# Two transformer layers on one core: scan inputs of the second mixer as 128-row products, values as a feature tile, and preparations moved into the first feed-forward

## The chip, the cores and the metric

One Trainium2 chip, one of its cores. The metric is the time of one execution on the device in microseconds (us), median of three. The core has TensorE (PE, with its weight loads as PEld), VectorE (DVE), ScalarE (ACT), GpSimd (POOL) and SyncE (SP, which here only issues DMAs). All tensors are float32; most products are done as three passes of a split operand (below).

## The reference, cut to what matters

The program is two layers over 512 tokens with 1024 features. The first (a mixer of four kinds of attention and convolution, then a feed-forward of width 2816) matters here only as the place where work for the second is done. The second layer is modulated by a vector c, and half of its mixer is an S5 scan:

```
mod = silu(c) @ w_mod + b_mod          # 6 x 1024: shift1, scale1, gate1, shift2, scale2, gate2
h   = rms(x) * norm1 * (1 + scale1) + shift1
u, q, k, v = split(h @ w_in)           # 512 scan features, 512 of queries, 128 keys, 128 values
a   = exp(dt * (lam_re + i lam_im))    # one complex pole per state, 32 groups x 64 states
bb  = (a - 1) / lam * b                # per group: 16 inputs -> 64 states
s[l] = a * s[l-1] + bb @ u[l]          # the scan
y[l] = Re(c @ s[l]) + d * u[l]
attention of 8 query heads on 2 key heads, window 128, with a learned bias by distance
x = x + gate1 * (norm(glu(gelu(y))), norm(attention)) @ w_out
x = x + gate2 * feed_forward(rms(x) * norm2 * (1 + scale2) + shift2)
```

## The kernel before, in words

Features lie on partitions, tokens along the row; x is 8 tiles of 128 x 512. A weight chunk is 128 x 2048 (1 MB). SP loads it (`load_chunk`, L113) into one of two slots, ACT rounds it (`round_chunk`, L121), DVE takes the rest (`rest_chunk`, L127), and PE does `split_mm` (L133 to L135), three products per tile. Counting semaphores `w_loaded`, `w_hi`, `w_lo`, `w_used` pass a chunk on. The order of each engine's work is written out by hand; an engine does its list strictly in order, and there is a barrier of all engines between stages.

The first feed-forward (`FeedForward`, L243) runs in two halves of 11 up turns (each a chunk for two tiles, 48 products) and 8 down turns (33 products): 38 turns, numbered from 0. In an up turn DVE copies both banks out of PSUM with the norm's root, takes the rest of the chunk two ahead, multiplies gate and value and takes `hlo`, the rest of the rounded product, which the down turns need. In the last down turns ACT squares x and POOL adds for the norm r3 of the second layer.

Beside it runs `Modulation` (L382). Its matrix is cut into 16 chunks of 384 columns, each 8 row blocks: 128 steps on DVE (L432, L435), 4 per up turn, 3 per down turn, into a ring of six accumulators. PE sums a finished chunk over its partitions by three products with a column of ones (`reduce`, L445), two turns after its last step in the first half; six of the 16 sums come after the feed-forward. `finish_early` and `finish` add the bias, the latter in the second mixer. SP loads half a chunk (`load`, L413) when the half two back is used up. POOL computes the poles and, when ACT has moved two transposed tiles (`a_moved`), the B matrices times the powers 0 to 3 of the pole (L1387), where time is taken in chunks of TS = 4 steps.

The second mixer is the stage at L1805. PE's order: the first chunk of w_in2 with the shifted norm as it comes (`shifted_dve`, `shifted_act`), a small product for the distance bias, transposes of B, the second chunk, `inputs(0)`, the third chunk (one feature tile, and the values with tokens on the partitions: 96 products of 128 columns), `inputs(1)`, the fourth and fifth chunk, `lag_weights`, and the attention in 16 pairs `p`, with the scan's outputs (`lags`, `from_states`) put between. `inputs(pair)` (L2272) makes the chunk inputs of the scan: for each of two tiles, real and imaginary part, each of four steps t and each of four 32-row groups one product, with the input read at a stride of four. DVE turns them by the angles (`spin`), scans (`scan`, L2129) and turns back (`spin_back`). The angles come from `turns` (ACT), `angle` (DVE), `sines` (ACT) and `cosine` (DVE) in this stage, and POOL lifts C by the powers (L1923, L1940). SP (L1890) loads C, a time table and two tables for the bias, then a weight chunk, writes 8 rows of the bias 128 times over to DRAM (`rel_scratch`, L1902) and reads them back skewed (`bias2`, L1908). PE's `lags` and `from_states` write the output at a stride of four.

Of the kernel before, what the change touches and what calls it, by code (L numbers as in the profile page):

```python
# [381 lines left out]
class Modulation:  # L382
# [3 lines left out]
    EARLY = 6  # L386
    AT_END = 10
    UP, DOWN = 4, 3

    def __init__(self, k, io, sb, ctx, pr, mods, keep_sem):  # L390
# [4 lines left out]
        self.ready, self.step, self.early = k.sem("mod_c_ready"), k.sem("mod_step"), k.sem("mod_early")  # L395
        self.reduced = keep_sem("mod_reduced")
        self.loaded = [k.sem("mod_loaded0"), k.sem("mod_loaded1")]
        self.at = 0

# [18 lines left out]

    def multiply(self, dve, steps):

        for e in range(self.at, min(self.at + steps, 8 * self.N)):
# [7 lines left out]
            if j == 0:  # L429
                if c >= self.KEPT:  # L430
                    dve.wait_ge(self.reduced, c - self.KEPT + 1)
# [6 lines left out]
        self.at += steps  # L438

    def reduce(self, pe, c):  # L440
        pe.wait_ge(self.step, 8 * (c + 1))
        if c == self.EARLY:
            pe.wait_ge(self.early, 1)
# [5 lines left out]
    def reduce_after(self, pe, turn):  # L449

        for c in range(self.AT_END):
            if turn == (self.turn_of(8 * (c + 1)) + 2 if c < self.EARLY else HALF + KT + 3 + 2 * (c - self.EARLY)):
                self.reduce(pe, c)

    def finish_early(self, dve):
        dve.wait_ge(self.reduced, self.EARLY)
        dve.tensor_tensor(self.mods[:, 0:16], self.k.bank[7][:, 0:16], self.pr("b_mod")[:, 0:16], ALU.add)\
            .then_inc(self.early, 1)

    def finish(self, dve):  # L460
        dve.wait_ge(self.reduced, self.N)
        return dve.tensor_tensor(self.mods[:, 16:48], self.k.bank[7][:, 16:48], self.pr("b_mod")[:, 16:48], ALU.add)
# [133 lines left out]
def program(nc, io):  # L596
    root_ctx = ExitStack()
    with root_ctx:
# [728 lines left out]
        ffn_ctx = ExitStack()  # L1327
        a_rows = sb("a_rows", [P, 2, S], ctx=ffn_ctx)
        xhi = nc.alloc_sbuf_tensor_at("xhi_ffn1", [P, KT, S], R, offset=o_at)
        xlo = sb("xlo_ffn1", [P, KT, S], R, ffn_ctx)  # L1330
        modulation = Modulation(k, io, sb, ffn_ctx, pr, mods, keep_sem)
# [16 lines left out]
        def out_bank(t):  # L1348
# [4 lines left out]
        b_in, col_exp, col_sin, col_den, col_inv, a_made, a_turned, a_moved = (  # L1353
            k.sem(f"ssm_{w}") for w in ("b_in", "exponents", "sines", "denominator", "inverse", "wide", "turned", "rows"))
# [7 lines left out]
        with nc.Block() as block:  # L1362

            @block.sync
            def _(sp):
# [5 lines left out]
                    .then_inc(b_in, 16)  # L1371
                for n in range(GU, IN2 + 4):
                    load_chunk(sp, k, n % 2, ffn.source(n) if n < IN2 else io["w_in2"][IN2_AT[n - IN2]], after_lo=n - 1)
                    for half in range(2, 2 * modulation.N):
                        if modulation.turn_of(4 * (half - 1)) == n - GU - 4:
                            modulation.load(sp, half)

            @block.gpsimd
            def _(pool):
# [56 lines left out]
                for n in range(1, TS):  # L1436
                    was, now = (powers[:, m, :, :, :].rearrange("p a t n -> p a (t n)") for m in (n - 1, n))
                    for a, op in ((0, ALU.subtract), (1, ALU.add)):
                        tt(twist[:, 0, :], was[:, 0, :], a_rows[:, a, :], ALU.mult)
                        tt(twist[:, 1, :], was[:, 1, :], a_rows[:, 1 - a, :], ALU.mult)  # L1440
                        tt(now[:, a, :], twist[:, 0, :], twist[:, 1, :], op)
                for j in range(1, KT - 1):
                    r3.add(pool, k, j)
# [3 lines left out]
            def _(act):  # L1447
# [76 lines left out]

                for half in range(2):
# [5 lines left out]
                    for j in range(KT):  # L1531
                        if half == 1:
                            if j == 0:
                                act.preload_act_table_set("natural_log_exp_and_others")
# [9 lines left out]
            def _(dve):  # L1544
# [103 lines left out]

                for half in range(2):
                    for i in range(HALF * half, HALF * half + HALF):  # L1650
                        ffn.dve_up(dve, i, k.root[:, :], lambda: modulation.multiply(dve, modulation.UP // 2))
                    for j in range(KT):
# [4 lines left out]
                        if half == 0 and j == KT - 1:  # L1657
                            modulation.finish_early(dve)
                        if half == 1 and j == 1:
                            dve.wait_ge(modulation.early, 1)  # L1660
                            dve.scalar_tensor_tensor(out=scale1, in0=scale1, scalar=1.0, in1=pr("norm1"), op0=ALU.add,
                                                     op1=ALU.mult)
# [3 lines left out]
            def _(pe):  # L1666
# [109 lines left out]
                for half in range(2):  # L1776
                    for i in range(HALF * half, HALF * half + HALF):
# [11 lines left out]
                        modulation.reduce_after(pe, turn)  # L1789
                        turn += 1  # L1790
                    for j in range(KT):
                        ffn.pe_down(pe, half, j)
                        modulation.reduce_after(pe, turn)
                        turn += 1
                r3.pe_sum(pe, k, KT - 2, [KT - 1])
                for n in range(modulation.AT_END, modulation.N):
                    modulation.reduce(pe, n)
# [8 lines left out]
        bt = sb("b_turned", [P, 2, S], ctx=mix_ctx)  # L1806
        proj2 = sb("proj2", [P, 9, S], ctx=mix_ctx)
        v2 = sb("v2", [P, NT, P], ctx=mix_ctx)
        y = o_all
        lift = sb("c_lifted", [P, 2, 16, TS + 1, 32], ctx=mix_ctx)  # L1810
        circle = sb("cos_sin", [P, 16, 2, NCK], ctx=mix_ctx)
# [3 lines left out]
        kx2 = sb("kx2", [P, S], ctx=mix_ctx)  # L1815
        k.nmax = sb("nmax2", [P, 32], ctx=mix_ctx)
# [4 lines left out]
        ssm_c = over("ssm_c", [P, 2, 16, 32], bias_at)  # L1821
        time = over("time", [P, S], bias_at + 2 * TILE)
        hot = over("hot", [33, 384], bias_at + 3 * TILE)
# [6 lines left out]
        states = [over("states0", [P, 2, 8, NCK], raw_at + 4 * TILE),  # L1830
                  powers[:, 0:2, :, :, :].rearrange("p n a t c -> p n (a t) c")]
# [4 lines left out]
        hot_in, rel_made, rel_sb, rel_out, rel_in, c_taken, time_set = (  # L1836
            k.sem(w) for w in ("hot_in", "rel_made", "rel_copied", "rel_out", "rel_in", "ssm_c_taken", "time_set"))
        h3_scaled, h3_rounded, h3_split = k.sem("in2_scaled"), k.sem("in2_rounded"), k.sem("in2_split")
        evac2a, evac2v, half_made, c_in, bt_made, bt_sb, lifted, turned, angled, sined, half_sined, circled = (
            k.sem(w) for w in ("in2_stored_a", "in2_stored_v", "in2_half", "ssm_c_in", "b_turned", "b_copied", "c_lifted",  # L1840
                               "turns", "angles", "sines", "half_sines", "circle"))
# [12 lines left out]
        chunk_time = time[:, :].rearrange("p (c t) -> p c t", t=TS)[:, :, 0]  # L1854
        clock = k.bank[6][:, 0:NCK]
# [9 lines left out]
        SPIN_AT = (1, 3, 5, 7, 9, 11)  # L1865
# [929 lines left out]
```

## Time and profile before

| | us |
|---|---|
| median of three executions | 1278.69 (1277.31 to 1279.43) |
| the profiled execution, its own time | 1280.15 |
| span from its first to its last instruction | 1278.4 |
| PE busy in it | 1228.0 |
| mean granted clock of TensorE | 0.984 of full |

The page gives busy times by engine, the costliest groups of instructions and the DMA issues. A line of the timeline is one or several like instructions: start, length, engine, source line, operation, output and inputs, count, and in brackets the idle time of the engine ahead of it with what ended it. PE's products overlap in the records: the start of the next tells how long one took. PE's counts give two records for a float32 product of the scan or the attention. Some matmul records can be missing.

### The profile page before, as it was taken

To read this page: it belongs to the slowest core of one execution; us is meant where nothing else is said; L and a number is where in the kernel's file an instruction comes from. 1 tells how busy PE (TensorE), PEld (TensorE's weight loads), DVE (VectorE), ACT (ScalarE), POOL (GpSimd) and SP (SyncE) were. 2 spreads that over 40 slices of the span, in tenths; PEclk is the share of its full clock that TensorE was granted. 3 is DMA by queue.
4 is the path that set the end of the run, shared out by engine and by line. 5 is a ranking of instruction groups with operands and counts; after the bars stand their busy time and mean duration, and the time that the engine had idled before them with its cause. 6 is when DMAs were issued, how large, how long until landed. Compare 5 with 4: busy or idle time off the path is not lost. (4 is left out here: it accounts for less than half of the span.)

```text
span 1278.4 us, 15375 instructions
## 1 busy us (share of the span) xinstructions
PE 1228.0 (96%) x6230; PEld 964.9 (75%) x6230; DVE 762.3 (60%) x1224; ACT 485.6 (38%) x738; POOL 125.3 (10%) x124
## 2 busy tenths in 40 slices
PE   7999998899999999999997999879899999999998
PEld 5786665578888788888885785558688878888877
DVE  5536674755665865656555896846755652455542
ACT  5244545734322212222324814564433331333320
POOL 0000000014000800000010930014100000000000
PEclk9999999999999999999998998979899999999999
DMA  9311011222443365554443341102122223222222
GB/s 345 130 62 66 34 66 47 86 100 99 166 153 132 118 206 190 173 173 135 134 154 121 62 88 34 67 6 95 66 99 99 78 73 127 101 99 99 68 91 89
DMA packets 25829, 138.40 MB, mean 108 GB/s; under 512 B 2879, under 2 KB 5152, under 8 KB 16544
## 3 DMA queue, kind: packets, MB, share of 16 engines
q1 hardware_dynamic: 25760, 137.43, 32.0%
q8 instruction: 49, 0.80, 0.3%
q14 instruction: 20, 0.16, 0.0%
HBM read 133.75 MB, written 3.67 MB: 107 GB/s over the span
## 5 line engine op out<-in xcount | busy, mean ns | idle before, releaser
L133 PE MATMUL bank<-xhi_ffn,w_hi_part 128*128 128x512 f32 x704 | 278.1, 395 | 4.4 <-DVE xlo_ffn L233 4.4
L134 PE MATMUL bank<-xlo_ffn,w_hi_part 128*128 128x512 f32 x704 | 277.1, 394 | 0.0
L121 ACT ACTIVATE w_hi_part<-w_raw 128x2048 fp32r<-128x2048 f32 (+1 forms) x96 | 165.8, 1727 | 290.6 <-PE bank L135 288.9
L135 PE MATMUL bank<-xhi_ffn,w_lo_part 128*128 128x512 f32 x704 | 275.2, 391 | 0.0
L127 DVE TENSOR_TENSOR w_lo_part<-w_raw,w_hi_part 128x2048 fp32r<-128x2048 f32 (+1 forms) x96 | 198.4, 2067 | 111.8 <-ACT w_hi_part L121 107.6
L133 PEld LDWEIGHTS bank<-xhi_ffn,w_hi_part 128*128 128x128 f32 x704 | 133.0, 189 | 34.7 <-issue 5.4
L135 PEld LDWEIGHTS bank<-xhi_ffn,w_lo_part 128*128 128x128 f32 x704 | 132.8, 189 | 29.5
L134 PEld LDWEIGHTS bank<-xlo_ffn,w_hi_part 128*128 128x128 f32 x704 | 132.6, 188 | 28.0 <-issue 0.2
L360 DVE SCALAR_TENSOR_TENSOR squares<-bank,param,squares 128x511 f32<-128x511 f32 x88 | 63.9, 747 | 84.7 <-ACT squares L343 83.1
L133 PE MATMUL bank<-hhi,w_hi_part 128*128 128x512 f32 x240 | 94.5, 394 | 1.7 <-DVE hlo L368 1.7
L133 PE MATMUL bank<-hhi_half,w_hi_part 128*128 128x512 f32 x240 | 94.2, 392 | 0.7 <-DVE hlo_half L332 0.7
L134 PE MATMUL bank<-hlo,w_hi_part 128*128 128x512 f32 x240 | 93.4, 389 | 0.0
L134 PE MATMUL bank<-hlo_half,w_hi_part 128*128 128x512 f32 x240 | 93.4, 389 | 0.0
L135 PE MATMUL bank<-hhi,w_lo_part 128*128 128x512 f32 x240 | 93.4, 389 | 0.0
L135 PE MATMUL bank<-hhi_half,w_lo_part 128*128 128x512 f32 x240 | 93.4, 389 | 0.0
L435 DVE SCALAR_TENSOR_TENSOR mod_acc<-mod_w,mod_c,mod_acc 128x384 f32<-128x384 f32 x112 | 75.6, 675 | 2.7
L133 PE MATMUL bank<-xhi,w_hi_part 128*128 128x512 f32 x144 | 61.4, 427 | 8.4 <-DVE w_lo_part L954 7.4
L343 ACT ACTIVATE squares<-bank,param 128x512 f32<-128x512 f32 x44 | 31.9, 777 | 82.8 <-PE bank L135 82.8
L320 DVE TENSOR_TENSOR squares<-bank,rms_root 128x512 f32<-128x512 f32 x22 | 15.2, 691 | 79.7 <-PE bank L135 72.4
L135 PE MATMUL bank<-xhi,w_lo_part 128*128 128x512 f32 x144 | 57.3, 398 | 0.0
L134 PE MATMUL bank<-xlo,w_hi_part 128*128 128x512 f32 x144 | 56.9, 395 | 0.0
L133 PEld LDWEIGHTS bank<-hhi_half,w_hi_part 128*128 128x128 f32 x240 | 45.1, 188 | 12.8 <-issue 1.7
(363 smaller groups left out, 1928.5 us busy)
## 6 DMA issues: line engine op xcount, KB each, us to landing
mod_w<-in_w_mod SPq DMA_DIRECT2D x32, 768.0 KB, 4.4
w_raw<-in_w_gu SPq DMA_DIRECT2D x22, 1024.0 KB, 4.8
w_raw<-in_w_down SPq DMA_DIRECT2D x32, 704.0 KB, 4.1
w_raw<-in_w_up SPq DMA_DIRECT2D x22, 1024.0 KB, 4.8
w_raw<-in_w_in_f SPq DMA_DIRECT2D x8, 1024.0 KB, 5.1
w_raw<-in_w_out SPq DMA_DIRECT2D x8, 1024.0 KB, 4.9
w_raw<-in_w_in SPq DMA_DIRECT2D x5, 1024.0 KB, 4.8
x<-in_x SPq DMA_DIRECT2D x8, 256.0 KB, 6.5
```

The lines of the kernel that those rows point to most:

```text
L121: act.activation(k.whi[:, slot, 0:width], k.raw[:, slot, 0:width], ACT.Copy).then_inc(k.w_hi, 1)
L127: dve.tensor_tensor(k.wlo[:, slot, 0:width], k.raw[:, slot, 0:width], k.whi[:, slot, 0:width].bitcast(F), ALU.subtract).then_inc(k.w_lo, 1)
L133: pe.matmul(out, whi, xhi, start=first, stop=False)
L134: pe.matmul(out, whi, xlo, start=False, stop=False)
L135: return pe.matmul(out, wlo, xhi, start=False, stop=last)
L320: dve.tensor_tensor(gate, k.bank[a][:, :], root, ALU.mult).then_inc(self.gated, 1)
L343: act.activation(k.sq[:, s, :], k.bank[s][:, :], ACT.Identity, bias=bias[:, 2 * i + a:2 * i + a + 1], scale=taps[:, 6 * i + 3 * a + 2:6 * ...
L360: dve.scalar_tensor_tensor(out=y, in0=k.bank[s][:, 0:S - back], scalar=taps[:, tap:tap + 1], in1=y, op0=ALU.mult, op1=ALU.add).then_inc(se ...
L435: ins = dve.scalar_tensor_tensor(out=acc, in0=w, scalar=self.c[:, j:j + 1], in1=acc, op0=ALU.mult, op1=ALU.add)
```

## The change

- Modulation: 6 steps per up turn and 5 per down turn, so that step 128 falls in turn 22. PE sums four chunks at once into four 32-row groups of bank 7 (`reduce(m)`, each with a 32-column weight that holds a column of ones at place m), one turn after their last step (turns 6, 11, 17, 23). In turn 23 DVE copies the bank, in 24 PE transposes it and DVE adds the bias and forms both scales.
- The lift of C (POOL), the angles, sines and cosines (ACT, DVE) are done in the first feed-forward: POOL from turn 24, ACT and DVE in the last down turns. C and the time table are loaded there.
- `inputs(pair)`: the rows of the four steps are laid under each other by DMA from SBUF to SBUF, 32 DMAs for the powers at the stage's start, 16 per pair for the inputs; then 16 products of 128 rows per pair. The scan tiles of `proj2` are stored by step (t outer), so `lags` and `from_states` have no stride and the output of DVE has one.
- Values: 24 products of 512 columns into a feature tile, copied by ACT, four transposes by PE.
- `lag_weights` and ACT's copies of its result come right after `inputs(0)`; one third of a back rotation moves from pair 11 to ahead of the attention; the first `load` of SP comes after `rel_scratch`.

The core of the diff:

```diff
 class Modulation:
-    UP, DOWN = 4, 3
+    UP, DOWN = 6, 5
+    GROUP = 4
...
-    def reduce(self, pe, c):
-        pe.wait_ge(self.step, 8 * (c + 1))
...
-        for t in range(3):
-            mm = pe.matmul(self.k.bank[7][:, 3 * c + t:3 * c + t + 1], self.acc[:, c % self.KEPT, P * t:P * t + P],
-                           self.k.ones[:, 0:1], start=True, stop=True)
+    def reduce(self, pe, m):
+        pe.wait_ge(self.step, 8 * self.GROUP * (m + 1))
+        for q in range(self.GROUP):
+            mm = pe.matmul(self.k.bank[7][32 * q:32 * q + 32, 0:self.W], self.pick[:, 32 - m:64 - m],
+                           self.acc[:, (self.GROUP * m + q) % self.KEPT, :], start=(m == 0), stop=(m == 3))
         mm.then_inc(self.reduced, 1)
+    def pe_after(self, pe, turn):
+        for m in range(4):
+            if turn == self.turn_of(8 * self.GROUP * (m + 1)) + 1:
+                if m == 0:
+                    pe.wait_ge(self.picks, 2)
+                self.reduce(pe, m)
+        if turn == self.summed_at + 1:
+            pe.wait_ge(self.copied, 1)
+            for t in range(3):
+                mm = pe.transpose(self.k.bank[7][:, P * t:P * t + P], self.acc[:, 0, P * t:P * t + P], self.k.ident)
+            mm.then_inc(self.turned, 1)
...
 # first feed-forward, ACT, second half
                     for j in range(KT):
+                        if half == 0 or j < KT - 1:
+                            ffn.act_weights(act, ffn.down_chunk(half, j) + 2)
                         if half == 1:
...
                             r3.act_square(act, k, x[:, j, :], j)
-                        if half == 0 or j < KT - 1:
-                            ffn.act_weights(act, ffn.down_chunk(half, j) + 2)
+                            if j == 0:
...
+                                turns(0)
+                                turns(1)
+                            if j in (1, 2):
+                                turns(j + 1)
+                            if 2 <= j < 6:
+                                sines(j - 2)
...
                 r3.act_root(act, KT, eps_col[:, 0:1])
-                act.preload_act_table_set("trig_and_small")
...
 # DVE
+                            if 1 <= j < 5:
+                                angle(j - 1)
+                            if 3 <= j < 7:
+                                cosine(j - 3)
...
 # second mixer, SP
+                for pair in range(2):
+                    for t in range(TS):
+                        for q in range(4):
+                            sp.dma_start(b_rows[pair][rows_of(t), q, :, :, :],
+                                         powers[rows_of(q), TS - 1 - t, :, 2 * pair:2 * pair + 2, :])\
+                                .then_inc(b_rows_in[pair], 16)
+                def turn_inputs(pair):
+                    sp.wait_ge(evac2a, pair + 1)
+                    sp.wait_ge(evac2v, pair + 1)
+                    for t in range(TS):
+                        for q in range(4):
+                            sp.dma_start(u_rows[rows_of(t), 2 * pair:2 * pair + 2, q, :],
+                                         proj2[rows_of(q), 2 * pair:2 * pair + 2, NCK * t:NCK * t + NCK])\
+                                .then_inc(u_rows_in[pair], 16)
+                sp.wait_ge(b_rows_in[0], 256)
+                sp.wait_ge(b_rows_in[1], 256)
+                turn_inputs(0)
                 sp.wait_ge(rel_sb, 1)
                 sp.dma_start(io["rel_scratch"], rel_rows[:, :].unsqueeze(1).broadcast_to([8, P, 384])).then_inc(rel_out, 16)
+                load_chunk(sp, k, (IN2 + 4) % 2, io["w_in2"][IN2_AT[4]], after_lo=IN2 + 3)
+                turn_inputs(1)
...
 # PE
                 def inputs(pair):
-                    for b in (2 * pair, 2 * pair + 1):
+                    pe.wait_ge(b_rows_in[pair], 256)
+                    pe.wait_ge(u_rows_in[pair], 256)
+                    for b in range(2):
                         for a in range(2):
-                            for t in range(TS):
-                                for q in range(4):
...
-                                    mm = pe.matmul(in_banks[q][:, at:at + NCK], powers[r, TS - 1 - t, a, b, :],
-                                                   steps_of(r, b)[:, :, t], start=(t == 0), stop=(t == TS - 1))
+                            for q in range(4):
+                                at = NCK * (2 * b + a)
+                                mm = pe.matmul(in_banks[q][:, at:at + NCK], b_rows[pair][:, q, a, b, :],
+                                               u_rows[:, 2 * pair + b, q, :], start=True, stop=True)
                     mm.then_inc(v_made, 1)
...
                 features(IN2 + 1, 0).then_inc(half_made, 1)
-                pe.wait_ge(evac2v, 1)
-                features(IN2 + 1, 1).then_inc(k.w_used, 1)
                 pe.wait_ge(rel_sb, 1)
                 pe.wait_ge(bt_sb, 2)
                 inputs(0)
+                lag_weights()
+                pe.wait_ge(evac2v, 1)
+                features(IN2 + 1, 1).then_inc(k.w_used, 1)
+                pe.wait_ge(k.w_lo, IN2 + 3)
                 pe.wait_ge(evac2a, 2)
-                features(n, 0).then_inc(half_made, 1)
-                pe.wait_ge(evac2v, 2)
...
+                features(IN2 + 2, 0).then_inc(half_made, 1)
                 pe.wait_ge(v_turned, 4)
                 inputs(1)
+                pe.wait_ge(evac2v, 2)
+                features(IN2 + 2, 1).then_inc(k.w_used, 1)
...
                 features(IN2 + 3, 0).then_inc(half_made, 1)
+                pe.wait_ge(values_sb, 1)
+                for i in range(NT):
+                    mm = pe.transpose(k.bank[7][:, P * i:P * i + P], v_wide[:, P * i:P * i + P], k.ident)
+                mm.then_inc(values_turned, 1)
                 features(IN2 + 3, 1).then_inc(k.w_used, 1)
```

## Rows read from the trace of the kernel before

**Rows 1.** The page, first part: busy us (share of the span) xinstructions.

```profile
PE 1228.0 (96%) x6230; PEld 964.9 (75%) x6230; DVE 762.3 (60%) x1224; ACT 485.6 (38%) x738; POOL 125.3 (10%) x124
```

**Rows 2.** Waits of PE: who waited for whom, us in total, times, longest.

```profile
PE bank L133 <- DVE xlo_in L233: 7.6, 1, 7.6
```

**Rows 3.** Windows, second mixer: length, busy PE, PEld, DVE, ACT, POOL, clock, DMA share, GB/s.

```profile
720.91:728.42 7.51, 7.51 (x129) 6.99 (x128) 7.41 (x17) 7.39 (x11) 7.12 (x6) 1.00 0.47 59
...
734.12:744.88 10.76, 10.76 (x98) 10.69 (x96) 10.69 (x15) 1.23 (x2) 10.13 (x9) 1.00 0.45 53
...
752.39:763.60 11.21, 11.21 (x53) 9.13 (x50) 10.44 (x29) 1.23 (x2) 0.00 (x0) 1.00 0.40 132
...
780.68:839.53 58.85, 50.75 (x479) 31.01 (x478) 41.69 (x154) 32.31 (x91) 0.51 (x1) 0.90 0.10 37
```

**Rows 4.** Timeline of DVE in turns 9 and 10 (start, length, what).

```profile
425.14 3.21 DVE L435 SCALAR_TENSOR_TENSOR mod_acc<-mod_w,mod_c,mod_acc 128x384 f32<-128x384 f32 x2
...
440.04 1.01 DVE L332 TENSOR_TENSOR hlo_half<-squares,hhi_half 128x512 fp32r<-128x512 f32 x1 [0.70 <-ACT hhi_half L313]
```

**Rows 5.** Timeline of POOL, B powers: first and last rows of 18 operations.

```profile
417.98 3.01 POOL L1387 TENSOR_TENSOR ssm_products<-b_powers,a_rows 128x512 f32<-128x512 f32 x2 [99.48 <-issue]
...
446.77 1.48 POOL L1387 TENSOR_TENSOR b_powers<-ssm_products 128x512 f32<-128x512 f32 x1
```

**Rows 6.** Timeline of PE, end of the first down turn (turn 11).

```profile
441.10 0.50 PE L133 MATMUL bank<-hhi_half,w_hi_part 128*128 128x512 f32 x1 [0.65 <-DVE hlo_half L332]
...
441.90 0.72 PE L445 MATMUL bank<-ones,mod_acc 128*128 128x1 f32 x6
442.49 0.47 PE L133 MATMUL bank<-hhi_half,w_hi_part 128*128 128x512 f32 x1
442.81 0.39 PE L134 MATMUL bank<-hlo_half,w_hi_part 128*128 128x512 f32 x1
```

**Rows 7.** Timeline of DVE, an up turn without POOL: its first, middle, last.

```profile
529.16 0.69 DVE L320 TENSOR_TENSOR squares<-bank,rms_root 128x512 f32<-128x512 f32 x1 [3.42 <-PE bank L135]
...
533.38 1.27 DVE L435 SCALAR_TENSOR_TENSOR mod_acc<-mod_w,mod_c,mod_acc 128x384 f32<-128x384 f32 x2
...
536.34 0.69 DVE L332 TENSOR_TENSOR hlo_half<-squares,hhi_half 128x512 fp32r<-128x512 f32 x1
```

**Rows 8.** Timeline of SP: two DMAs issued one after the other.

```profile
2.11 0.43 SPq L822 DMA_DIRECT2D x<-in_x  x1
2.58 0.43 SPq L820 DMA_DIRECT2D x<-in_x  x1
```

**Rows 9.** DMA issues: count, KB each, median us from issue to landing.

```profile
spread<-in_spread SPq DMA_DIRECT2D x4, 16.0 KB, 13.0
...
param<-in_param SPq DMA_DIRECT2D x1, 4.0 KB, 1.8
```

**Rows 10.** Timeline of SP around rel_scratch; L1908 waits until it is done.

```profile
715.66 0.80 SPq L1902 DMA_DIRECT2D rel_scratch<-rel_rows  x1
748.79 0.42 SPq L1908 DMA_DIRECT2D bias<-rel_scratch  x1
```

**Rows 11.** Windows, two us inside that write, columns as in rows 3.

```profile
736.00:738.00 2.00, 2.00 (x21) 2.00 (x19) 1.97 (x4) 0.00 (x0) 1.92 (x2) 1.00 0.44 51
```

**Rows 12.** Timeline of PE: transposes of B, lag weights, one set of lags.

```profile
708.07 1.09 PE L2364 MATMUL bank<-kept,b_powers 128*128 128x128 f32 x8
...
777.22 2.02 PE L2296 MATMUL bank<-c_lifted,b_turned 128*32 128x128 f32 x64
...
802.02 2.68 PE L2308 MATMUL bank<-proj,lag_weights 128*128 128x512 f32 x8
```

**Rows 13.** Windows, the clock as PE stands and after, columns as in rows 3.

```profile
687.00:688.00 1.00, 0.00 (x0) 0.00 (x0) 0.34 (x1) 0.62 (x1) 0.00 (x0) 0.71 0.00 0
...
697.00:698.00 1.00, 1.00 (x5) 0.76 (x4) 1.00 (x3) 0.40 (x2) 0.00 (x0) 0.67 0.00 0
```

**Rows 14.** Timeline of ACT at the stage boundary.

```profile
684.42 1.28 ACT L1540 ACT_TABLE_LOAD   x1
```

More of the change, by code:

```diff
@@ new lines, in dve_after @@
+    def dve_after(self, dve, chain, turn):
+        if turn == self.summed_at:
+            dve.wait_ge(self.reduced, 4)
+            dve.tensor_copy(self.acc[:, 0, :], self.k.bank[7][:, 0:self.W]).then_inc(self.copied, 1)
+        if turn == self.summed_at + 1:
+            dve.wait_ge(self.turned, 1)
+            chain.link(dve.tensor_tensor(
+                self.mods[:, :].rearrange("p (m q t) -> p m q t", m=4, q=4),
+                self.k.bank[7][:, 0:self.W].rearrange("p (t q r) -> p r q t", t=3, q=4)[:, 0:4, :, :],
+                self.pr("b_mod").rearrange("p (m q t) -> p m q t", m=4, q=4), ALU.add))
+            for n, norm in ((1, "norm1"), (4, "norm2")):
+                scale = self.mods[:, 8 * n:8 * n + 8]
+                ins = dve.scalar_tensor_tensor(out=scale, in0=scale, scalar=1.0, in1=self.pr(norm), op0=ALU.add,
+                                               op1=ALU.mult)
+            ins.then_inc(self.done, 1)
@@ L1352, in program @@
         g_ffn = pr("g_ffn")
[L1353 to L1354 removed]
+        b_in, col_exp, col_sin, col_den, col_inv, a_made, a_turned, a_moved, powers_made, c_in, lifted = (
+            k.sem(f"ssm_{w}") for w in ("b_in", "exponents", "sines", "denominator", "inverse", "wide", "turned", "rows",
+                                        "powers_made", "c_in", "c_lifted"))
+        time_in, time_set, turned, angled, sined, half_sined, circled = (
+            k.sem(f"circle_{w}") for w in ("time_in", "time_set", "turns", "angles", "sines", "half_sines", "cosines"))
+        time = over("time", [P, S], time_at)
+        angles = over("angles", [P, 4, S], o_at)
+        half_sines = over("half_sines", [P, 2, S], o_at + 4 * TILE)
+        circle = over("cos_sin", [P, 16, 2, NCK], circle_at)
+        lift = over("c_lifted", [P, 2, 16, TS + 1, 32], lift_at)
+        ssm_c = over("ssm_c", [P, 2, 16, 32], rows_at)
+        chunk_time = time[:, :].rearrange("p (c t) -> p c t", t=TS)[:, :, 0]
+        clock = k.bank[6][:, 0:NCK]
         def col(n):
@@ L1647, in _, with angle, cosine @@
                 dve.wait_ge(r2.inverted, 1)
+                def angle(b):
+                    ang = angles[:, b, :]
+                    dve.wait_ge(turned, b + 1)
+                    for part, op in ((TH_HI, ALU.subtract), (TH_LO, ALU.add)):
+                        for q in range(4):
+                            a = ang[:, NCK * q:NCK * q + NCK]
+                            mark = chain.mark(dve.scalar_tensor_tensor(
+                                out=a, in0=clock, scalar=col(part)[:, 4 * b + q:4 * b + q + 1], in1=a,
+                                op0=ALU.mult, op1=op))
+                        chain.need(mark)
+                    dve.tensor_scalar(ang, ang, 0.5, -0.5, ALU.min, ALU.max).then_inc(angled, 1)
+                def cosine(b):
+                    dve.wait_ge(half_sined, b + 1)
+                    half_sine = half_sines[:, b % 2, :].rearrange("p (t c) -> p t c", c=NCK)
+                    dve.tensor_scalar(circle[:, 4 * b:4 * b + 4, 0, :], half_sine, -2.0, 1.0, ALU.mult, ALU.add)\
+                        .then_inc(circled, 1)
+                modulation.set_picks(dve)
+                turn = 0
                 for half in range(2):
@@ L1656, in _ @@
                         modulation.multiply(dve, modulation.DOWN)
[L1657 to L1662, printed above, removed]
+                        if half == 1:
+                            if j == 1:
+                                dve.wait_ge(time_in, 16)
+                                dve.wait_ge(a_moved, 2)
+                                dve.tensor_copy(clock, chunk_time).then_inc(time_set, 1)
+                                dve.wait_ge(time_set, 1)
+                            if 1 <= j < 5:
+                                angle(j - 1)
+                            if 3 <= j < 7:
+                                cosine(j - 3)
+                        modulation.dve_after(dve, chain, turn)
+                        turn += 1
+                own.dve = chain.n
                 ffn.dve_weights(dve, ffn.down_chunk(1, KT - 1) + 2)
@@ L2107, in spin @@
                     dve.wait_ge(v_made, pair + 1)
-                    dve.wait_ge(circled, 4)
                     if pair:
@@ L2222, in _ @@
                     spin_back(0, part)
+                for part in range(3):
+                    spin_back(1, part)
                 next_rest(GLU)
```

311 lines of the change are left out of this document (127 added, 184 removed).

## The prediction

> **What bounds the kernel now.** I read the page first: PE is busy 1228.0 of 1278.4 us, every other engine far less [rows 1]. PE's waits, next, are short and scattered; the longest is 7.6 us at the start of the second mixer [rows 2]. So PE's stream sets the end; an edit pays by what it takes off PE or out of a wait, and costs where it makes PE wait. The windows give the second mixer: scan inputs, values and projections to 763.6 us with PE never idle, then the attention, 58.85 us with PE busy 50.75 [rows 3]. The timelines of DVE, POOL, PE and SP then show where PE is only just served, and the reader is to see three things. (1) While POOL makes the B powers (18 operations, 417.98 to 448.3) DVE's two-input operations take 1.6 us instead of 0.62, and the last hlo of the first half is 0.65 us late for PE [rows 4 to 7]. (2) SP issues a DMA in 0.43 us, 0.47 apart [rows 8], and a small one behind large ones lands late [rows 9]. (3) The write of rel_scratch, issued at 715.66, is over only at 748.79; in between the DMA engines move 51 GB/s at a share of 0.44 [rows 10, 11].
>
> **The change, part by part.** Times are those of the profiled execution: its own time is 1280.15, its span 1278.4 (1.75 us lie around it), the median of the runs 1278.69. I add to 1280.15 and take off 1.46 at the end.
>
> *Modulation sums on PE.* Before: 16 reductions, ten of them inside the feed-forward at 0.59 and a late restart of 0.09, 0.68 us each [rows 6]; six behind it. After: four, each of four 32-column products with 384 columns. 32 such products with 128 columns took 2.02 us [rows 12], so 12 of them 0.76; I take 0.8 (bound above 3.2, the lag products' 0.27 per 128 columns one after another), and 0.55 for three transposes (8 took 1.09). Up to the end of turn 9 three old ones go for one new: -1.2. After turn 11 five old (3.4) go for two new and the transposes (2.15): -1.25.
>
> *More multiplications per turn (6 and 5, not 4 and 3).* Away from POOL, DVE's turn takes 7.9 us of PE's 11.1, each multiplication 0.62 [rows 7]; two more make 9.1: no cost. Turns 9 and 10 lie in POOL's stretch. PE ends turn 9 at 421.9 - 1.2 = 420.7. DVE then: copies from PSUM 1.2, wait 0.2, weights 1.8 (423.9), three multiplications at 1.57 (428.6), product 1.7, three more (435.0), hlo 1.7 (436.7). Turn 10: 1.2, weights 1.6 (439.5), product 1.75, ACT's rounding 0.7, hlo 1.3: 443.3. PE began its first down chunk at 431.8 and wants that hlo at 438.7: it stands 4.6. It ends the chunk at 444.2 and then meets the new second reduction, which wants multiplication 64: the fourth of the six that DVE does after the hlo. Three at 1.57 and, POOL being done near 448, one at 0.6: 448.6. PE stands 4.4 more and starts the second down chunk at 449.4; before, at 442.49 [rows 6]. That is +6.9, with the -1.2 in it (bounds: +1 if POOL's hold falls on other operations, +10 if on all). The next weights are ready at 452, wanted at 457: no third stall.
>
> A standing PE loses its clock. It stood from 687: the granted clock was 0.71 of full in 687 to 688, then 0.50 (1.2 of 2.4 GHz), and was back at 697.3, 2.8 us after work began at 694.5 [rows 13]. Four us at half rate cost +2.0 (bounds 0, 3.5).
>
> *Angles, sines, cosines, lifts and scales into the feed-forward.* By their durations in the mixer ACT gets at most 7.6 us of work in one of the last down turns, DVE 7.5, of PE's 7.5, and in both the weights stand first: hidden by PE's products, 0 (to +1 if a turn spills over; nothing to gain, as PE waited there for none of it). POOL's 30 operations (42.5 us before) begin in turn 24, some 56 us ahead of its next duty, and DVE has no multiplications left by then: 0. SP's two loads go out in idle time.
>
> *Stage boundary.* Between r3's sum and the mixer stood ACT's roots, a table load of 1.28 [rows 14], a weight rounding, DVE's rest, the barrier. The load goes: -1.28, in the next total. The six late reductions ended 3 us ahead of DVE's rest: their removal is worth 0.
>
> *Scan inputs.* Before, 64 products of 32 rows took 7.51 a pair [rows 3]; now 16 of 128 rows. Bounds 1.9 (16 of the old at 0.117) and 4.3 (16 at the lag products' 0.27: 1280 columns in 2.68 [rows 12]); I take 3.7, nearer to the lags, which have 128 rows too. What is added: SP issues 32 DMAs for the powers, waits for all, then 16 per pair behind the copies out of PSUM, and PE waits for 256 on each. Pair 0: SP starts at 690.8 with two small ones; 32 x 0.46 brings 706.3, landed 708.3 (4 KB alone took 1.8 [rows 9]); 16 more end at 716, landed 718. PE: start 693.26, first chunk and small work to 707.9 (0.5 waiting for ACT gone), half chunk 713.5. It stands 4.5, then does the 16 products and the lag weights (2.0) with 2.3 lost to the low clock: 726.0. Two half chunks: 737.2. DVE's spin lies beside them.
>
> Pair 1: its DMAs go out from 732, but SP issued rel_scratch at 716.9 and a 1 MB load before. rel_scratch takes 31 us (to 748), the load on the same engines 3, the rows 2.5: 753.5. The four 16 KB tables behind a 2 MB load took 13.0 us against 1.8 for 4 KB alone [rows 9]. PE stands 16.3 (bounds 3 and 19), the 16 products 6.0 at the low clock, half chunk 5.8: 765.3.
>
> The Trainium skill, DMA: Bandwidth & Descriptors, section Queues, rings and completion order, has all DMAs that SP issues share one ring on each of 16 engines, read in order. By it pair 1 can't pass rel_scratch: the sum made here; without it, rival A's. Its section on why a DMA increments its semaphore by 16 puts an 8-row source on 8 engines, with which the share of 0.44 agrees.
>
> *Values as a feature tile.* 96 products took 10.76 [rows 3]; now 24 of 512 columns at 0.232 (5.6, in the half chunk just counted) and four transposes 0.6 later on. Half chunk 770.9, transposes 771.5, half chunk 777.1. Before: 763.6. So +13.5 at this mark. The lag weights are gone from behind it: -2.0. DVE's scans and key scale just keep up.
>
> *Attention.* The lag products lose their stride (2.2 for 2.68, four times), ACT's 2.4 us of lag copies leave its start, a third of a back rotation leaves DVE; PE's idle there is 8.1 [rows 3]. I take -3.0 (bounds -7, and +1.5 if DVE's strided output takes twice its 0.74).
>
> Sum: +6.9 + 2.0 - 1.25 + 13.5 - 2.0 - 3.0 = +16.15: 1296.3 for this execution, 1294.8 beside the median.
>
> **Rivals.**
> A. *Pair 1's rows don't wait for rel_scratch.* For it: the share of 0.44 leaves half of the engines free. Against: a transfer over all engines needs the busy ones too, and the 13.0 us. They land at 731.6 + 0.7 + 7.5 + 2 = 742, a stall of 4.8 for 16.3: -11.5, 1283.
> B. *DVE keeps up in turns 9 and 10.* For it: POOL has just 18 operations to hold DVE with, however much DVE does. Against: DVE was 0.65 late already with less to do. Then -1.2 for +6.9 and no clock loss: -10.1, 1285.
> C. *Faster: the laid-out rows are nearly in time.* SP issues without gaps (0.43) and rel_scratch blocks nothing. Pair 0 lands at 716.3 (stall 2.8), pair 1 costs 4.0. With no stall in the mixer PE is 12.3 ahead at the mark instead of 13.5 behind, and the total is -9.65 (1269); with 6.8 of stalls -2.9, 1276. It decides where the mixer's stalls with their clock loss come to under 9.65 us; in my sum they are 25.8. For it: 7.6 + 4.6 us of PE's work do go there, and the slow write need not hold anyone. Against: 48 issues and two landings before pair 0.
>
> **How the numbers follow.** Forecast 0.52, A 0.16, B 0.09, C 0.23 (also A and B together, 1273). No change, within 0.2% or 2.6 us (about what a measurement of this kernel tells from none), is the upper part of C and little else: 0.07; faster 0.21, slower 0.72. The forecast's own range is 1288 to 1303. The given one goes down over B, A and most of C: 1271 to 1303.
>
> **What would show it.** In the trace after: PE idle near 439 and 444 us, released by DVE's hlo and its multiplications; some 4 us of PE idle before the first and 16 before the second group of scan input products, released by DMA, with a low granted clock behind each; these groups 3 to 6 us long; no table load at the boundary; attention near 56 us. The prediction is wrong if the second group starts within 5 us of the half chunk ahead (A or C), or if the second down chunk begins before 444 (B).

## The result

The changed kernel takes 1314.34 us, the kernel before 1278.63: ratio 1.0271, 95% interval 1.0253 to 1.0289, slower by 35 us. The profiled execution took 1314.91 us, its span is 1313.1. The forecast was 1295 us, from 1271 to 1303: the direction is right, the size is not, and the time lies outside the range. One of the four executions took 4235.91 us, for a reason that nothing here shows: the ratio leaves it out, and the median of the other three is 1313.76.

The page after, first part:

```profile
PE 1220.3 (93%) x5909; PEld 950.4 (72%) x5909; DVE 766.1 (58%) x1226; ACT 483.0 (37%) x737; POOL 134.9 (10%) x124
```

PE works 7.7 us less than before [rows 1] and stands 42 us more. Its waits after (who waited for whom, us in total, times, longest; [rows 2] is the second line's before):

```profile
PE bank L2328 <- DMA b_powers<-proj: 31.4, 2, 19.8
PE bank L133 <- DVE xlo_in L233: 10.1, 1, 10.1
PE bank L2391 <- DVE prob L2250: 7.6, 6, 2.5
PE bank L133 <- DVE hlo_half L332: 5.0, 1, 5.0
PE bank L452 <- DVE mod_acc L443: 3.6, 1, 3.6
```

The first is new, as are the last two. Cut at the same points of PE's timeline, the two spans differ like this (us):

| stretch | before | after | difference | forecast |
|---|---|---|---|---|
| first feed-forward to the end of r3's sum | 683.01 | 689.83 | +6.8 | +7.65 |
| from there to the mixer's first product | 11.53 | 10.08 | -1.45 | -1.28 |
| to the mark (end of the fourth projection chunk) | 69.06 | 95.1 | +26.1 | +14.8 |
| to the first scores | 17.1 | 17.1 | 0 | -2.0 |
| attention | 58.85 | 61.3 | +2.5 | -3.0 |
| last stage | 438.9 | 439.6 | +0.7 | 0 |

*Feed-forward*, timeline of PE after (start, length, what, in brackets the idle time ahead and who ended it), for [rows 6]:

```profile
441.38 0.80 PE L133 MATMUL bank<-hhi_half,w_hi_part 128*128 128x512 f32 x1 [5.04 <-DVE hlo_half L332]
446.65 1.51 PE L452 MATMUL bank<-mod_acc,mod_pick 128*32 128x384 f32 x8 [3.63 <-DVE mod_acc L443]
448.09 0.80 PE L133 MATMUL bank<-hhi_half,w_hi_part 128*128 128x512 f32 x1
```

The two waits stand where they were expected, 5.04 and 3.63 us for 4.6 and 4.4; the 0.80 of the product at 448.09, 0.47 before, is the low clock.

*Mixer front*, the same view at the two groups of scan inputs and at the lag weights, then the timeline of SP:

```profile
732.75 5.49 PE L2328 MATMUL bank<-b_powers,b_rows 128*128 128x128 f32 x32 [11.56 <-DMA b_powers<-proj]
738.17 2.02 PE L2350 MATMUL bank<-c_lifted,b_turned 128*32 128x128 f32 x64
771.39 6.59 PE L2328 MATMUL bank<-b_powers,b_rows 128*128 128x128 f32 x32 [19.80 <-DMA b_powers<-proj]
```

```profile
698.17 21.51 SPq L2017 DMA_DIRECT2D b_rows<-b_powers  x32
721.17 10.17 SPq L2026 DMA_DIRECT2D b_powers<-proj  x16
731.38 0.76 SPq L2034 DMA_DIRECT2D rel_scratch<-rel_rows  x1
732.20 5.61 SPq L113 DMA_DIRECT2D w_raw<-in_w_in  x1
746.79 23.22 SPq L2026 DMA_DIRECT2D b_powers<-proj  x16
```

A copy is issued in 0.67 us (21.51 / 32) or 0.64 (10.17 / 16); I had counted 0.46. The last 16 took 1.45 each: SP itself was held back, behind rel_scratch. The clock follows the waits (windows as in [rows 3]; the clock is the number before the DMA share):

```profile
724.00:727.00 3.00, 0.00 (x0) 0.00 (x0) 0.00 (x0) 0.00 (x0) 0.00 (x0) 0.84 0.23 49
727.00:730.00 3.00, 0.00 (x0) 0.00 (x0) 0.00 (x0) 0.00 (x0) 0.00 (x0) 0.50 0.24 50
733.00:736.00 3.00, 3.00 (x15) 3.00 (x16) 0.00 (x0) 0.00 (x0) 0.00 (x0) 0.50 0.43 50
736.00:739.00 3.00, 3.00 (x49) 2.88 (x50) 0.72 (x3) 0.00 (x0) 0.00 (x0) 0.95 0.64 80
812.16:873.49 61.33, 52.44 (x479) 31.92 (x478) 41.33 (x151) 29.88 (x87) 0.00 (x0) 0.86 0.06 18
```

With PE idle from 721.2 the clock falls from 2.4 to 1.2 GHz (0.50), and the first group runs at that level until 736.3, 3.5 of its 5.5 us; the second, begun at 771.39, until 777.2. The rest of the first group, at the full clock:

```profile
736.29:738.07 1.78, 1.78 (x17) 1.76 (x16) 0.00 (x0) 0.00 (x0) 0.00 (x0) 1.00 0.45 52
```

Half of its 32 records take 1.8 us there, so a whole group would take about 3.6 (an estimate from this window). The last line of the windows before is the attention, the answer to that of [rows 3]: clock 0.86 for 0.90.

### The profile page after: what moved, and what is told of

It is laid out like the page before. It is cut to its first block and busy times, and to the rows that moved or that the text cites. A ratio compares the mean times of both kernels' runs of the same rounds, so it can differ in the third digit from the quotient of the medians.

```text
span 1313.1 us, 14793 instructions
## 1 busy us (share of the span) xinstructions
PE 1220.3 (93%) x5909; PEld 950.4 (72%) x5909; DVE 766.1 (58%) x1226; ACT 483.0 (37%) x737; POOL 134.9 (10%) x124
## 3 DMA queue, kind: packets, MB, share of 16 engines
q1 hardware_dynamic: 30880, 140.58, 31.7%
## 5 line engine op out<-in xcount | busy, mean ns | idle before, releaser
L133 PEld LDWEIGHTS bank<-hhi,w_hi_part 128*128 128x128 f32 x240 | 45.0, 188 | 12.6 <-DVE hlo L368 2.5
```

Source lines behind the costliest of these rows:

```text
L133: pe.matmul(out, whi, xhi, start=first, stop=False)
```

## The experiments

All ratios are to the kernel before, each timed beside it on one chip.

| run | median us | ratio (95%) |
|---|---|---|
| products_of_32 | 1276.97 | 1.0015 (0.9981 to 1.0048) |
| step_order_alone | 1278.35 | 1.0000 (0.999 to 1.001) |
| broadcast_from_act | 1329.15 | 1.0398 (1.0383 to 1.0414) |
| powers_from_pool | 1320.24 | 1.0327 (1.0311 to 1.0343) |
| broadcast_last | 1301.19 | 1.0177 (1.0161 to 1.0192) |
| fewer_beside_pool | 1299.85 | 1.0165 (1.0145 to 1.0185) |
| second_sum_later | 1306.43 | 1.0226 (1.0209 to 1.0242) |
| products_and_fewer | 1266.36 | 0.9923 (0.9896 to 0.9951) |
| weights_rest_later | 1261.07 | 0.9900 (0.9860 to 0.9940) |

**products_of_32**

```
-  for t, q: sp.dma_start(b_rows[pair][...], powers[...]); sp.dma_start(u_rows[...], proj2[...])
-  mm = pe.matmul(..., b_rows[pair][:, q, a, b, :], u_rows[:, 2 * pair + b, q, :])
+  for t in range(TS): mm = pe.matmul(..., powers[r, TS - 1 - t, a, b, :],
+                                     proj2[r, b, NCK * t:NCK * t + NCK], start=(t == 0), ...)
+  states = [powers[:, :, :, 2 * pair:2 * pair + 2, :] with n and a merged, for pair in range(2)]
```

> The changed kernel with its 16 products of 128 rows per pair and all 64 layout DMAs taken out again: 64 products of 32 rows per pair, as before, on the step-ordered projections; everything else of the change stays (lag weights early, values as a feature tile, the feed-forward part). Theory (the layout DMAs are the mixer's whole loss): the two DMA waits of 11.6 and 19.8 us and the low clock behind them go, each pair takes 7.5 us again, from the mixer's first product to the mark 66 to 67 us instead of 95.1 (69.1 before, lag weights +2.0, values -4.5), the attention falls from 61.3 to below 59, and the time is 1283 to 1286 us: what is then left over the kernel before is the feed-forward's 6.8. Rival (the strided evictions or the new order on DVE hold the mixer as well): over 75 us to the mark, time above 1292.

Measured 1276.97, 37 us off the changed kernel and 6 below the low end of what was expected. Timeline of PE, the first pair, and the windows to the mark and of the attention:

```profile
721.16 3.85 PE L2304 MATMUL bank<-proj,b_powers 32*128 32x128 f32 x128
```

```profile
699.86:759.25 59.39, 59.39 (x527) 48.30 (x528) 38.83 (x78) 17.65 (x23) 1.81 (x1) 0.95 0.40 83
776.72:839.51 62.79, 54.78 (x479) 32.51 (x478) 41.55 (x151) 29.95 (x87) 0.00 (x0) 0.80 0.05 18
```

The DMA waits, 31.4 us, were the mixer's loss. But the 64 products of 32 rows take 3.85 us here, not 7.51 [rows 3]: only the order of what they read differs, which the next run tests by itself. The laid-out 16 products took 5.5 and 6.6 us. To the mark it is 59.4 us for 69.06 before; the attention, against the expectation, is 4 us longer than before, which is taken up below.

**step_order_alone**

```
+  if tile < 4: act.activation(by_step(proj2[:, tile, :]), by_chunk(bank[:, :]), ACT.Copy)   (DVE's copy too)
-  steps_of(r, b)[:, :, t]
+  proj2[r, b, NCK * t:NCK * t + NCK]        (lags, from_states and output likewise, all on the kernel before)
```

> The kernel before with one part of the change alone: the four scan tiles are copied out of PSUM in step order (all first steps, then all second ones), so the scan input products, the lag products and the state products read and write without a stride; no layout DMAs, and nothing else of the change. Theory (the stride of the moving operand, not the 32 rows, made a pair of input products cost 7.5 us): both groups of 64 products take 3.9 us as in products_of_32, the four lag groups 2.42 for 2.68, and the time is 1269 to 1272 us. Rival (the 3.9 us there come from another order around them, or the strided copies and the strided output on DVE give it back): groups over 6 us, or time above 1276.

The groups took 3.85 us, as the theory said, and the time stayed, as the rival said: 1278.35. Windows to the mark, and where the gain went, timelines of DVE and PE:

```profile
692.39:754.15 61.76, 61.51 (x531) 51.90 (x532) 57.83 (x110) 33.84 (x51) 40.07 (x30) 0.97 0.40 88
```

```profile
757.94 2.63 DVE L2140 TENSOR_TENSOR_SCAN b_powers<-ssm_cols,b_powers 128x128 f32<-128x128 f32 x8
760.49 0.67 DVE L2096 COPY proj<-bank 128x512 f32<-128x512 f32 x1
761.21 1.06 PE L645 MATMUL bank<-square_sum,kept 128*32 128x512 f32 x1 [4.23 <-DVE proj L2096]
```

At the mark PE is 7.3 us shorter (61.76 for 69.06), the two halvings. DVE is busy 57.83 of these 61.76 us; it copies the next tile behind its scans, and PE waits 4.2 us for it and then runs at the low clock: from the mark to the first scores it takes 23.1 us for 17.1. The attention takes 59.6 us for 58.9. With the cosines off DVE, as in the change and in products_of_32, DVE is busy 38.83 of 59.39 and no such wait is left. So the step order doesn't pay alone; the cosines moved alone were not run.

**broadcast_from_act and powers_from_pool**

```
-  sp.wait_ge(rel_sb, 1); sp.dma_start(io["rel_scratch"], ...)
+  act.wait_ge(rel_sb, 1); act.dma_start(io["rel_scratch"], ...)      (both)
-  for pair in range(2): ... sp.dma_start(b_rows[pair], ...)
+  for pair in range(1): ... ;  pool.dma_start(b_rows[1], ...) x16    (powers_from_pool)
```

> The changed kernel with one edit: the write of rel_scratch (31 us on the DMA engines) is issued by ScalarE, in a ring of its own, and no longer stands in SyncE's ring ahead of the second pair's 16 row copies. Theory (order in SyncE's ring): the copies leave as fast as SyncE issues them, 16 x 0.65 = 10.4 us from about 746, so PE's second wait falls from 19.8 to 7 to 9 us and the time to 1301 to 1304. Rival (the DMA engines themselves are held by the broadcast, whichever ring it is in): the wait stays over 14 us, time above 1308. The first wait, 11.6 us, stays in both.

> The kernel of the run broadcast_from_act, and the 16 copies of the second pair's powers are issued by GpSimd in place of SyncE. Theory (the first wait is SyncE's issue time, 32 x 0.67 + 16 x 0.64 us one after another): SyncE reaches the first pair's rows some 10 us earlier, unless GpSimd takes over 1.3 us for each; PE's first wait falls from 11.6 to 2 to 6 us and the time by 6 to 9 us, to 1293 to 1297. Rival (the engines' bandwidth or the landing of small copies sets it): the copies share the same 16 engines, the first wait stays over 9 us and the time above 1300.

Both of my theories failed here: 15 and 6 us slower than the changed kernel. (A ring is the queue of the DMAs that one engine has issued.) SP's timeline in powers_from_pool, and ACT's issue of the broadcast:

```profile
696.85 11.16 SPq L2017 DMA_DIRECT2D b_rows<-b_powers  x16
712.71 36.80 SPq L2026 DMA_DIRECT2D b_powers<-proj  x16
```

```profile
714.63 1.36 ACTq L2103 DMA_DIRECT2D rel_scratch<-rel_rows  x1
```

The powers left as planned (GpSimd issued its 16 in 8.66 us), and SP reached the first rows 8.5 us earlier. Then the broadcast, in ScalarE's ring, went out 2 us behind them, and the 16 copies in SyncE's ring took 36.8 us to issue; PE stood 31.7 us before the first group, 40.5 in broadcast_from_act. The second waits were 6.8 us in both, just under the 7 to 9 expected: by then the broadcast was over. So it isn't the order within a ring that holds the copies.

**broadcast_last**

```
   turn_inputs(1)
+  sp.wait_ge(rel_sb, 1); sp.dma_start(io["rel_scratch"], ...)
-  v_wide = over(..., kx2_at);  act.wait_ge(rel_out, 16)
+  v_wide = sb(...)                                 (b_rows[1] from GpSimd, as above)
```

> The changed kernel with the layout DMAs kept, the second pair's powers issued by GpSimd, and the write of rel_scratch issued by SyncE only behind the second pair's rows (values_by_feature has a place of its own for that). Theory (the broadcast from 8 rows holds half of the DMA engines for 31 us, and every copy that starts during it waits, in whichever ring): with nothing beside them 16 row copies take 10.2 us of issue and 2 of landing; PE's first wait is 4 to 7 us, the second 6 to 8, and the time 1294 to 1298 us. Rival (the copies are slow by themselves, SyncE's ring full of small ones): a wait of 12 us or more is left, time above 1303.

PE's waits are 5.13 and 6.83 us, inside both intervals: copies that meet no broadcast cost what their issue costs. The time missed, 1301.2 for 1294 to 1298: SP waits for the broadcast before it loads the gate's weights, ACT stands before those weights in its queue, and PE waits for ACT's squares instead.

```profile
PE bank L2331 <- DMA b_powers<-proj: 12.0, 2, 6.8
PE bank L667 <- ACT square_sum L2073: 6.7, 1, 6.7
PE bank L667 <- ACT square_b L2073: 3.0, 1, 3.0
```

**copies_alone**

```
+  16 x dma_start(new[32 rows, 2 runs of 128], old[32 rows, 2 runs of 128])   behind the last store, SyncE
+  16 x (1 run of 256);  16 x (128 partitions, 1 run of 128);  16 x (from HBM, 32 rows, 1 run of 256)
+  broadcast, 16 x on SyncE;  broadcast, 16 x on ScalarE;  broadcast from 16 rows
```

> The kernel before, with DMAs added behind its last store, when nothing else runs, each group after the last has landed; its time is read only from the groups. (1) 16 copies of 32 partitions with two runs of 512 B, the change's row copies, from SyncE; (2) the same bytes as one run of 1 KB; (3) 16 copies of 128 partitions, one run of 512 B; (4) 16 loads of 32 rows from HBM, one run of 1 KB; (5) the broadcast of rel_scratch, then group 1 behind it in SyncE's ring; (6) the broadcast, and group 1 from ScalarE's ring; (7) the broadcast with 16 source rows of 64 copies in place of 8 rows of 128. Theory: group 1 takes 0.64 us of issue each with nothing beside it, so it is the price of such a DMA and no contention; (2) shows whether it goes by runs (then about 0.45) or not; in (5) and (6) alike the 16 copies are over only when the broadcast is, 30 us; in (7) it takes about 16 us, since twice the DMA engines carry it. Rival (order in one ring): (6) has its copies landed within 14 us of its start. Rival (HBM's write rate sets the broadcast): (7) takes 30 us as well.

The kernel was executed once (1414.83 us; only the groups are read). Timelines of SP and ACT, one line a group, in the order of the expectation:

```profile
1274.56 10.28 SPq L2481 DMA_DIRECT2D w_raw<-w_raw  x16
1286.12 10.32 SPq L2492 DMA_DIRECT2D w_raw<-w_raw  x16
1297.69 10.18 SPq L2496 DMA_DIRECT2D w_raw<-w_raw  x16
1309.18 7.31 SPq L2500 DMA_DIRECT2D w_raw<-in_time  x16
1317.83 0.80 SPq L2486 DMA_DIRECT2D rel_scratch<-w_raw  x1
1318.67 37.21 SPq L2481 DMA_DIRECT2D w_raw<-w_raw  x16
1357.19 0.71 SPq L2486 DMA_DIRECT2D rel_scratch<-w_raw  x1
1395.54 0.59 SPq L2511 DMA_DIRECT2D rel_scratch<-w_raw  x1
```

```profile
1357.98 36.19 ACTq L2584 DMA_DIRECT2D w_raw<-w_raw  x16
```

A copy from SBUF (the core's on-chip memory) to SBUF is issued in 0.64 us whether it has one run or two and 32 partitions or 128; a load from HBM in 0.46, which was my number. Behind the broadcast 16 copies take 36 to 37 us from either ring, 2.3 us each. They are slowed and not shut out: from ScalarE's ring a copy lands a median of 4.8 us after its issue, for 1.9 with nothing beside it. The broadcast from 16 rows is over by the end of the span, 1413.0, 17.5 us after its issue, for the 33.1 of [rows 10]: the same bytes from twice the rows take about half the time. The DMA view of 1270 to 1413 shows it too, GB/s in 40 slices of 3.6 us, mostly 51 to 60 during the first two broadcasts and 102 in the last:

```profile
GB/s 26 65 55 48 34 51 53 37 96 106 92 55 71 33 51 52 55 56 55 52 56 55 75 48 32 56 56 56 57 55 54 60 60 65 55 58 102 102 102 76
```

So HBM's write rate does not set the 51 GB/s of the first two.

**fewer_beside_pool and second_sum_later**

```
-  UP, DOWN = 6, 5
+  def steps(self, turn): return {8: 4, 9: 2, 10: 2}.get(turn, 6)             (fewer_beside_pool)
-  if turn == self.turn_of(8 * self.GROUP * (m + 1)) + 1:
+  if turn == self.turn_of(8 * self.GROUP * (m + 1)) + (2 if m == 1 else 1):  (second_sum_later)
```

> The changed kernel with the modulation's steps dealt out anew: 6 a turn, but 4, 2 and 2 in turns 8, 9 and 10, while GpSimd makes the powers; the second sum so comes two turns later. Theory (the feed-forward's loss is the 5.0 us wait for the last hlo of the first half and the 3.6 us wait for the second sum, both of DVE's multiplications beside GpSimd's): both waits fall below 1 us, r3's sum ends at 681 to 683 us of the span, and the time falls by 7 to 9 us to 1305 to 1307. Rival (DVE has no room anywhere, the 128 steps only push the wait to another turn): waits of 3 us or more for DVE in turns 12 to 24, time above 1311.

> The changed kernel with the second modulation sum alone moved one turn later. Theory: its wait of 3.6 us (the 64th multiplication is late for it) goes, the 5.0 us wait for hlo stays, time 1309.5 to 1311.5. Rival (PE only waits later, since DVE stands behind it in the next turn anyway, with the third group's accumulators waiting for this sum): a wait of 2.5 us or more appears in the next three turns, time above 1312.5.

Both waits are gone in the first, 0.8 us being left of the wait for hlo; in the second the 3.6 alone. Both gained more than I expected, 14.5 us (for 7 to 9) and 7.9 (for 3 to 5); from 1313.76 it is 13.9 and 7.3. The clock is part of it, windows of the changed kernel, second_sum_later and fewer_beside_pool:

```profile
440.00:460.00 20.00, 14.99 (x53) 10.72 (x54) 13.26 (x16) 3.07 (x3) 5.29 (x4) 0.68 0.45 151
```

```profile
440.00:460.00 20.00, 18.14 (x73) 14.04 (x74) 17.43 (x22) 3.39 (x3) 5.81 (x4) 0.83 0.51 168
```

```profile
440.00:460.00 20.00, 20.00 (x93) 15.82 (x92) 18.13 (x21) 3.45 (x3) 6.24 (x4) 1.00 0.73 249
```

At the mixer's first product the profiled executions are 10.5 and 4.4 us ahead of the changed kernel, of which 7.9 and 3.6 are waits. Over the whole execution they are 12.3 and 8.9 us shorter, so 1.8 and 4.5 us lie behind that point. In second_sum_later 3.1 of them are the attention (58.3 us for 61.3), which the edit doesn't touch; there the clock stayed at the full level after a wait of 2.5 us:

```profile
847.41 0.65 PE L2391 MATMUL bank<-kept,prob 128*128 128x128 f32 x4 [2.46 <-DVE prob L2250]
848.62 2.42 PE L2360 MATMUL bank<-proj,lag_weights 128*128 128x512 f32 x8
```

What is left I can't assign.

**products_and_fewer and weights_rest_later**

The first holds both edits above. The second adds one:

```
-  if p == 8: next_rest(OUT2)
+  if p == 12: next_rest(OUT2)
```

> The changed kernel with both repairs: the products of 32 rows of products_of_32 in place of the layout DMAs, and the steps dealt out as in fewer_beside_pool. Theory (the two losses are separate): 1277.0 less the 14.5 us that fewer_beside_pool gained, 1262 to 1267 us, 1% below the kernel before. Rival (part of the 14.5 came from stalls that only the layout DMAs had, their clock above all): 1268 to 1272.

> The kernel of products_and_fewer, with DVE's subtraction for the second output chunk (2.3 us) at pair 12 of the attention in place of pair 8. Theory (the attention did not get shorter because DVE bounds it at pairs 8 to 10: PE waits 2.46 us for prob, falls to the low clock, and the fourth lag products take 4.6 us for 2.4): the wait falls below 1 us, the clock stays, and the time is 3 to 4.5 us below 1266.4, at 1262 to 1263.5. Rival (another engine is as late there, or the subtraction is missed at the start of the last stage): a wait over 1.5 us stays or appears at the gate product, time over 1265.

1266.36 lies at the upper end of the theory's 1262 to 1267 and below the rival. Against products_of_32 it gains 10.6 us, not the 14.5 of fewer_beside_pool. 1261.07 is 1 us better than expected and the fastest here, 1.0% below the kernel before. The intervals of these two runs overlap; what tells them apart is the trace, where the attention takes 55.1 us for 59.8. Why the attention had not shortened, timelines of PE in the changed kernel and in weights_rest_later, wait ahead of the fourth lag products and these products:

```profile
852.58 1.11 PE L2391 MATMUL bank<-kept,prob 128*128 128x128 f32 x4 [2.45 <-DVE prob L2250]
854.78 4.57 PE L2360 MATMUL bank<-proj,lag_weights 128*128 128x512 f32 x8
```

```profile
801.75 0.66 PE L2370 MATMUL bank<-kept,prob 128*128 128x128 f32 x4 [0.26 <-DVE prob L2226]
802.96 2.42 PE L2339 MATMUL bank<-proj,lag_weights 128*128 128x512 f32 x8
```

The changed kernel's window ahead of that wait:

```profile
843.00:851.00 8.00, 7.13 (x98) 4.88 (x94) 7.82 (x22) 3.66 (x11) 0.00 (x0) 1.00 0.34 110
```

DVE, busy 7.82 of 8 us, bounded that stretch; PE, faster by the strides, waited for it, lost its clock and took 4.6 us for 2.4 of work. The wait does not bring the low clock each time: of the nine traces with a wait of 2.3 to 2.5 us there, seven have these products at 4.35 to 4.62 us, fewer_beside_pool at 3.6 and second_sum_later at 2.42. What decides it stays open. The best three of these kernels each have single executions 9 to 15 us over their median; their intervals hold them, their cause is open.

## Why the prediction was wrong

- *Waits in the feed-forward and the clock behind them* (+7.65 forecast, +6.8 measured): right, both waits within 0.8 us, and shown by taking them out.
- *Stage boundary* (-1.28, -1.45): right, and the trace after has no table load there.
- *Scan inputs, pair 0*: this is the step that failed. "32 x 0.46", from a load out of HBM [rows 8], priced a copy within SBUF, which takes 0.64 to 0.67. The powers' 32 took 21.5 us for 14.7, the first 16 rows 10.2 for 7.5: PE stood 11.6 us for 4.5. powers_from_pool and broadcast_last took 16 copies off SP, and it reached the first rows some 8 us earlier. The right price adds 7.1 us to the sum, about 1303 for this execution (an estimate), still short of 1314.9: the terms of the attention and the lag weights, below, failed too.
- *Pair 1*: that rel_scratch would hold the rows is right, and its wait of 16.3 came out 19.8. That SP issued everything later is not why, since PE's own work came as much later (rel_scratch 14.5 us behind the forecast, the half chunk's end 14.4). I had given 31 us from rel_scratch's issue to its end, where [rows 10] has 33.1 and broadcast_last 32.5, and 5.5 from there to the products, which became 7.5 (estimate: 731.38 + 32.5 = 763.9, to 771.39). My reason was too narrow. If the order in one ring were the reason, another ring would have freed them, and it didn't: what holds them is the broadcast from 8 rows in the DMA engines that all rings share, for 33 us [rows 10]. The Trainium skill has this rule too, on the same page (DMA: Bandwidth & Descriptors, Issuing engines are not separate DMA queues): all issuers' DMAs run on the same 16 engines. The runs agree, and that 16 rows took about half the time agrees with 8 rows on 8 engines.
- *Products of 128 rows*: the size is right. 3.7 us was forecast at the full clock, for about 3.6; with the low clock 8.0 for the first group and the lag weights, measured 7.4, and 6.0 for the second, measured 6.4. What was wrong is the gain. The 7.51 us that they were to replace were mostly stride: without it the old ones take 3.85, and there was next to nothing for the layout to win, even at the full clock. I had overlooked a rule: by the Trainium skill, SBUF — State Buffer, Door 1: The DMA port swizzle, each access that goes on to another 16-byte line costs extra, and four-byte elements 16 bytes apart do so every time. The runs agree (7.51 and 3.85).
- *Values as a feature tile*: right as read from the trace, where the three half chunks and the four transposes behind the second group take 17.3 us for 17.6; no run tests it alone.
- *Lag weights gone from behind the mark* (-2.0, 0): they had covered ACT's square_b, for which PE now waits 1.4 us.
- *Attention* (-3.0, +2.5): the stride's gain, 0.26 us a group, is there (2.42 for 2.68) but brought PE to DVE's bound at pairs 8 to 10, where its wait grew from 1.9 to 2.5 us, and the clock took more than the gain back. weights_rest_later, with that wait at 0.26, has an attention of 55.1 us, near the forecast's 56.

Rival A (rows not held by rel_scratch), B and C are all out. The two DMA waits are 31.4 us for 20.8: 10.6 of the 18.6 us by which the sum fell short; attention and lag weights are 7.5 more.

## What to carry to other kernels

Price a DMA by its source: a small copy within SBUF cost SyncE 0.64 us in all three shapes tried, so 64 of them are 41 us of its time, and a broadcast from 8 rows slowed them to 2.3 us each, from SyncE as from ScalarE. Before laying operands out anew, take the stride out of the moving operand first. When PE gets faster in a stretch, read the next engine's busy time there: a wait of 2.5 us cost another 2 by the clock in seven of nine traces.

## What was unexpected in the hardware

- 64 products of 32 rows and 128 columns: 7.51 us when the columns lie 16 bytes apart, 3.85 when they lie together.
- Issue of a DMA from SyncE: 0.64 us from SBUF to SBUF, 0.46 from HBM; GpSimd issued such copies in 0.54 each (8.66 / 16).
- The same wait of 2.5 us was followed by TensorE at 1.2 GHz (granted clock 0.50) in the changed kernel and at 2.4 (1.00) in second_sum_later: lag products 4.57 and 2.42 us.
- 1.5 MB from 8 rows: 33 us, and small copies beside it are slowed, from SyncE's ring or ScalarE's (16 of them 36 to 37 us for 10.3); from 16 rows at most 17.5 us.
